# Expert key and value tiles fetched in pairs: one 1 MB transfer of 8 KB packets in place of two of 512 KB, into six slots managed as three pairs

## What is computed

```python
def peer_ffn(x, w_q, sub_k1, sub_k2, u_tab, v_tab):
    q = (x @ w_q).astype(f32).reshape(bsz, seq, PEER_HEADS, 2, PEER_KEY_DIM)
    s1 = jnp.einsum('bshd,hnd->bshn', q[..., 0, :], sub_k1.astype(f32))
    s2 = jnp.einsum('bshd,hnd->bshn', q[..., 1, :], sub_k2.astype(f32))
    v1, i1 = lax.top_k(s1, PEER_TOPK)
    v2, i2 = lax.top_k(s2, PEER_TOPK)
    ...
    def chunk(args):
        xc, ec, gc = args
        u = u_tab[ec].astype(f32)
        act = jax.nn.gelu(jnp.einsum('ced,cd->ce', u, xc.astype(f32))) * gc
        return jnp.einsum('ce,ced->cd', act, v_tab[ec].astype(f32)).astype(x.dtype)
```

## Time and profile before

| | us |
|---|---|
| median of 3 runs | 1951.95 (1950.99 to 1952.47) |
| the profiled execution | 1955.38 |
| its span | 1953.7 |
| TensorE busy | 1803.8 (92%) |
| VectorE busy | 926.1 (47%) |
| ScalarE busy | 430.0 (22%) |
| GpSimd busy | 428.6 (22%) |
| transfers issued from SyncE | 482.88 MB, 62.2% of the 16 DMA engines' time |
| gathers issued from GpSimd | 134.23 MB, 17.0% |

### The profile page before, as it was taken

One profiled execution on the slowest core, in us unless ns is written; L12 is line 12 of the kernel. 1 busy time (PEld: TensorE's weight loads), 2 busy tenths in 40 slices (PEclk: granted clock), 3 DMA queues, 4 the chain that ended last, 5 costly groups with the idle time before them and its releaser, 6 DMA issues. The chain is left out here.

```text
span 1953.7 us, 23396 instructions
## 1 busy us (share of the span) xinstructions
PE 1803.8 (92%) x9228; PEld 1174.7 (60%) x9228; DVE 926.1 (47%) x1973; ACT 430.0 (22%) x823; POOL 428.6 (22%) x312
## 2 busy tenths in 40 slices
PE   4988999888999999988899999989699999999998
PEld 4974443237787744323686558978588885444443
DVE  4467311123567742111699634976766663222222
ACT  5462110014345321001421434201110010000001
POOL 5820000015668400000300014212022112111110
PEclk9999899998999989999899999999899999999999
DMA  9886799994568579999532323599699999999996
GB/s 392 352 314 227 313 407 430 429 429 175 194 234 314 227 295 412 429 430 429 195 108 86 140 91 146 194 353 409 272 370 387 398 405 398 413 408 406 404 413 269
DMA packets 95088, 620.27 MB, mean 317 GB/s; under 512 B 11520, under 2 KB 12032, under 8 KB 60672
## 3 DMA queue, kind: packets, MB, share of 16 engines
q1 hardware_dynamic: 75824, 482.88, 62.2%
q0 software_dynamic: 18432, 134.23, 17.0%
q10 hardware_dynamic: 720, 1.61, 0.2%
HBM read 617.63 MB, written 1.05 MB: 317 GB/s over the span
## 5 line engine op out<-in xcount | busy, mean ns | idle before, releaser
L3032 PEld LDWEIGHTS bank<-peer_xT,peer_tiles_a 128*128 128x128 f32 x1376 | 164.5, 196 | 17.1 <-issue 11.1
L3032 PE MATMUL bank<-peer_xT,peer_tiles_a 128*128 128x128 f32 x1376 | 168.0, 280 | 2.6 <-DMA peer_tiles_a<-in_peer_u 2.5
L3081 PE MATMUL bank<-peer_tiles_a,peer_H 128*128 128x512 f32 x344 | 158.4, 597 | 9.5 <-DMA peer_tiles_a<-in_peer_v 7.5
L227 POOL TENSOR_TENSOR w_lo<-ring,w_hi 128x1024 fp32r<-128x1024 f32 x60 | 148.4, 2475 | 64.3 <-ACT w_hi L217 63.9
L3256 DVE CUSTOM_DVE_ANT_0 peer_junk<-peer_rows_b,bank 128x1024 bf16<-128x1024 f32 x64 | 78.1, 1220 | 172.4 <-issue 169.1
L1094 PE MATMUL bank<-ring,moe_slots 128*64 128x512 f32 x576 | 131.9, 608 | 14.9 <-DMA ring<-in_stream 14.9
L3052 PE MATMUL bank<-peer_x_rows_hi,peer_ident 128*128 128x512 f32 x256 | 129.7, 507 | 0.9 <-DVE peer_pre L3256 0.5
L1269 DVE TENSOR_TENSOR bank<-bank,mod 128x512 f32<-128x512 f32 x32 | 22.4, 700 | 221.2 <-PE bank L1144 221.2
L3081 PEld LDWEIGHTS bank<-peer_tiles_a,peer_H 128*128 128x128 f32 x344 | 63.8, 189 | 85.9 <-issue 70.0
L3256 DVE CUSTOM_DVE_ANT_0 peer_junk<-peer_rows_a,bank 128x1024 bf16<-128x1024 f32 x48 | 58.5, 1220 | 119.2 <-issue 114.6
L1094 PE MATMUL bank<-early,moe_slots 128*64 128x512 f32 x448 | 102.1, 597 | 11.7 <-DMA early<-in_stream 11.7
(11 more groups left out here) (518 smaller groups left out, 3566.2 us busy)
## 6 DMA issues: line engine op xcount, KB each, us to landing
ring<-in_stream SPq DMA_DIRECT2D x103, 2048.0 KB, 12.4
early<-in_stream SPq DMA_DIRECT2D x32, 2048.0 KB, 18.3
peer_tiles_a<-in_peer_u SPq DMA_DIRECT2D x86, 512.0 KB
peer_tiles_a<-in_peer_v SPq DMA_DIRECT2D x86, 512.0 KB
sb_mod_ring<-in_ada_t SPq DMA_DIRECT2D x64, 512.0 KB, 6.6
peer_tiles_b<-in_peer_u SPq DMA_DIRECT2D x42, 512.0 KB
peer_tiles_b<-in_peer_v SPq DMA_DIRECT2D x42, 512.0 KB
ret_mod_ring<-in_ada_t SPq DMA_DIRECT2D x32, 512.0 KB, 5.0
```

The costliest lines, as they stand in the source:

```text
L227: pool.tensor_tensor(self.shaped(self.w_lo, q, by_columns), self.quarter(n, q, by_columns), self.shaped(self.w_hi, q, by_columns).bitcast( ...
L3032: last = pe.matmul(K.bank[:, 2 + n // 4 % 2, n % 4 * P:(n % 4 + 1) * P], u[:, k, :], xT[:, k, :], start=(k == 0), stop=(k == KD - 1))
L3081: last = pe.matmul(K.bank[:, 2 + dh, :], H[:, m, :], first.slot(n)[:, dh * 512:(dh + 1) * 512], start=(m == 0), stop=(m == PK - 1))
```

## The change

Two neighbouring tiles are laid side by side in DRAM, so that for each partition 8 KB are contiguous, and one DMA brings both into two neighbouring slots. The six slots become three places of two; each place has one semaphore. SyncE waits until both tiles of a place are used. What TensorE, VectorE, ScalarE and GpSimd do, and in which order, is the same. All lines from L2911 on stand five lower in the changed file (the DMA is on L2916 there).

```diff
-        self.tile_in = [nc.alloc_semaphore(f"peer_tile_in{i}") for i in range(SLOTS)]
+        self.tile_in = [nc.alloc_semaphore(f"peer_tile_in{i}") for i in range(SLOTS // 2)]
...
-    def fetch(self, sp, n):
-        source = self.K_A["peer_u"][n] if n < PK else self.K_A["peer_v"][n - PK]
-        sp.dma_start(self.slot(n), source).then_inc(self.tile_in[n % SLOTS], 16)
+    def landed(self, n):
+        return self.tile_in[n // 2 % (SLOTS // 2)], 16 * (n // SLOTS + 1)
+
+    def fetch_two(self, sp, n):
+        source = self.K_A["peer_u"][n // 2] if n < PK else self.K_A["peer_v"][(n - PK) // 2]
+        i = n % SLOTS
+        room = self.tiles[0][:, i:i + 2, :] if i < FETCHED else self.tiles[1][:, i - FETCHED:i - FETCHED + 2, :]
+        sp.dma_start(room, source).then_inc(self.tile_in[n // 2 % (SLOTS // 2)], 16)
...
-            for n in range(FETCHED):
-                first.fetch(sp, n)
+            for n in range(0, FETCHED, 2):
+                first.fetch_two(sp, n)
...
-            for n in range(FETCHED, 2 * PK):
+            for n in range(FETCHED, 2 * PK, 2):
...
                 if n >= SLOTS:
-                    sp.wait_ge(tile_used, n - SLOTS + 1)
-                first.fetch(sp, n)
+                    sp.wait_ge(tile_used, n - SLOTS + 2)
+                first.fetch_two(sp, n)
...
             def keys(n):
-                pe.wait_ge(tile_in[n % SLOTS], 16 * (n // SLOTS + 1))
+                pe.wait_ge(*first.landed(n))
...
             def values(m):
                 n = PK + m
-                pe.wait_ge(tile_in[n % SLOTS], 16 * (n // SLOTS + 1))
+                pe.wait_ge(*first.landed(n))
...
-        "peer_u": a["peer_u_2"][0].reshape(P, P, KD, P).transpose(0, 3, 2, 1).reshape(P, P, KD * P),
-        "peer_v": a["peer_v_2"][0].reshape(P, P, D),
+        "peer_u": a["peer_u_2"][0].reshape(P, P, KD, P).transpose(0, 3, 2, 1).reshape(P // 2, 2, P, D)
+                  .transpose(0, 2, 1, 3),
+        "peer_v": a["peer_v_2"][0].reshape(P // 2, 2, P, D).transpose(0, 2, 1, 3),
```

## The result

| | before | the change |
|---|---|---|
| median of 5 runs | 1951.95 (1950.74 to 1956.61) | 1964.18 (1959.49 to 1966.19) |
| the profiled execution | 1955.38 | 1965.36 |
| its span | 1953.7 | 1963.7 |

What follows compares the result with a forecast made beforehand. TensorE sets the pace with DMA engines nearly full, waiting 12.1 us for tiles queued behind gathers. Terms -7.5 + 1 - 2.6 = -9.1 us took the median 1951.95 to 1943 us; 8-in-10 range 1938 to 1957.

Steps and rivals of the forecast that it cites:

- Packets: SyncE's tile queue: each pair goes as one 8 KB packet per partition, so 57,392 packets in place of 75,824.
- Share during a burst: Tiles beside gather bursts: turns by packet give each queue half of 409 GB/s, 205 for tiles in place of 139.
- rival B: Tiles beside gathers: their share stays at a third while depth falls; +17 to +43 us, 1969 to 1995; chance 0.09.
- Depth: Values part: a pair's slack falls from 12.3 to 9.8 us, its need is 6.9 to 8.5 us, so it fits.
- -7.5 + 1 in the values part: Values part: TensorE's 7 waits for value tiles go, -7.5 us, with 1 us of them left for small spare time.
- -2.6 in the picks part: Picks part: four key-tile waits of 4.6 us go, 2 us given back because VectorE's dots sit behind slower row gathers.
- Issue and waits: SyncE and TensorE: 128 DMAs in place of 256, and longer waits for two releases, were priced at nothing.
- Gathers' landing: Gathers beside the tiles: their median time to landing rises from 11.6 us to some 14.
- A: Gate part: gathered rows come late and hold TensorE up; whole kernel 1943 to 1977 us, centre 1960; chance 0.09.
- C: Values part: the DMA engines are the bound, waits move from tiles to rows; 1952 us within 3 us; chance 0.09.

Runs made afterwards that it cites:

- experiment 2: The kernel before with each gather split into two of 4 KB packets, tiles single: 1951.01 us, ratio 0.9989.
- experiment 8: The change with one place of two tiles in place of three, run once, so TensorE waits for every pair: 2781.28 us.
- experiment 7: The change with each pair as two DMAs of 4 KB packets on one semaphore, and gathers in 4 KB packets as well: 2013.22 us, ratio 1.0304.
- experiment 3: The change with a fourth place of two tiles (eight slots in place of six): 1940.73 us, ratio 0.9934 against the kernel before.
- experiments 9 and 10: The change (9) and the kernel before (10), each with 120 of 128 gathers left out: 1942.8 us and 1941.81 us.
- experiment 5: The kernel before with single tiles issued in twos after two releases, and gathers in 4 KB packets: 2006.51 us, ratio 1.0262.
- experiment 6: The change with each pair as two DMAs of 4 KB packets adding to the same semaphore: 2055.57 us, ratio 1.0493.

## Why the prediction was wrong

**Step by step.**

- *Packets*: right, 57,392 as forecast.
- *Share during a burst*: right, 211 GB/s for 205. The rule cited there from the Trainium skill (round robin at packet boundaries) agrees, and rival B is out. What failed is its worth: with single tiles an equal share moved the values part by 0.35 us (experiment 2).
- *Depth*: **the step that failed.** "6.9 to 8.5 us. It fits with 1.3 us or more to spare." The need was 9.5 to 11 us, because all that is not bytes was put at 1.6 us, after a transfer of 8 KB that had nothing beside it; beside gathers it is some 4.3, most of it ahead of the pair's first packet (experiment 8). The slack was put at 9.8 us, from a mean time per tile that held TensorE's waits and the value sums; where two tokens but no value sum fall among the four tiles it is 8.8, and for the late pairs it was 8.7 to 10.4. With the measured terms 5.1 + 4.3 = 9.4 is more than 8.8, even before anything is left of the pair ahead. The sign of the step hung on 1.3 us, and both its terms were put too favourably by about 1 us or more.
- *-7.5 + 1 in the values part*: measured +7.4, and waits for tiles of 9.7 us where about 1 was forecast, a rate of 385 GB/s for 405 and a part of 318 us for 306. The mistake beneath it: the seven waits of before had been priced, but not the tiles that just made it. Before, a tile had five tiles of slack and could be used when its own bytes were there; a pair loses a tile of slack and adds the bytes of its second tile to the first one's need (10.3 us of the part in experiment 7), and 19 times TensorE is held up by a little. Up to 1.7 of the 7.4 us are the lower clock, which no term of the sum held and which may be chance.
- *-2.6 in the picks part*: measured +1.8. TensorE waited 5.0 us for key tiles, not 0, and the longest wait was followed by the lower clock. That VectorE would follow where tiles are on time is right, as experiment 3 shows (-5.6).
- *Issue and waits at nothing*: right, experiments 9 and 10 differ by 1 us with intervals that overlap.
- *Gathers' landing "from 11.6 us to some 14"*: 12.7. With the fourth place it is 14.8.

**The rivals.** A names a cost in the gate part, but that part is 0.3 us longer: out. B is out, by the 211 GB/s. C is out: at 406 GB/s the fourth place carries the whole part, and the DMA share fell, it didn't stay at its limit. What came is a rival I had not written: the share moves as forecast, and the slack is too small for the new need. It was in the prediction as the depth step, but as a term with one sign in place of a range that crosses zero. The earlier trace rows had tiles of 524,288 bytes taking 10.84 to 13.19 us, where 3.8 us of rate and 1.6 us of landing explain half. That was no proof of a longer way, since most of the rest was other tiles of the same queue. While the tile issued at 1674.09 was on its way, its queue moved (packets, MB, share)

```profile
q1 hardware_dynamic: 465, 1.71, 35.5%
```

which is more than three tiles. But it was a reason not to trust 1.6 us: no row showed a way beside gathers with an empty queue ahead, and only experiment 8 does.

The range ended at 1957 and held no case for this.

## What to carry to other kernels

Merging transfers trades depth for share. Write down the slack (from issue to need, in the time the consumer takes without waits) and the need (all bytes of the merged transfer at the share it will get, and the time to its first packet and after its last, measured beside the same other traffic), and don't take the merge where they differ by less than the error of either. If a wide packet is worth having, find room for another place first: here the same pairs lost 0.5% with three places and gained 0.7% with four.

## What the runs showed of the hardware that was not expected

- Two queues that are both full share by the size of their packets: 139 GB/s for the tiles at 4 against 8 KB, 211 GB/s at 8 against 8 KB.
- A transfer of 1 MB took 2.2 us beyond its bytes when alone and about 4.3 us beside gathers. The growth lay ahead of its first packet (3.4 us after the issue in place of 0.96); from the last packet to landing it was 0.3 to 0.6 us in both cases.
- A wait cost TensorE about 0.3 us beyond what its row says (2.0 us for 7 waits, 5.5 us for 19), so many short waits are worse than few long ones of the same sum.
- A stretch of 3.4 us at a granted clock of 0.5 stood behind an idle time of 2.3 us in the picks part of the change, and behind the 2.1 us ahead of the first value tile in some kernels and not in others. Each made the run up to 1.7 us longer.
- With 4 KB gathers and tiles issued in twos TensorE was held up in steps of 2.1 us inside tiles that had landed, 23.2 us in the key tiles of experiment 5 and 18.1 us in those of experiment 7. No run tests the cause. The 4 KB gathers alone (experiment 2) did not show it, nor did the pairs alone.
- At a mean granted clock of 0.92, in the kernel of experiment 6 with its waits of up to 5.4 us, the same matmuls took 332.59 us for 300.94.
